# Gated heads of a two-stage transformer: level products on square tiles in column groups, inner levels through a compact table

## The reference

```python
def step(state, inp):
    qc, kc, vc, gc = inp
    bc = jnp.cumsum(gc, axis=2)
    diff = bc[:, :, :, None, :] - bc[:, :, None, :, :]
    decay = jnp.exp(jnp.where(causal, diff, -jnp.inf))
    scores = jnp.einsum('bhtd,bhsd,bhtsd->bhts', qc, kc, decay)
    o = jnp.einsum('bhts,bhsv->bhtv', scores, vc) + jnp.einsum('bhtd,bhdv->bhtv', qc * jnp.exp(bc), state)
    ...
```

## Time and profile before

| | before |
|---|---|
| median of 3 runs | 1345.93 us (1345.53 to 1348.4) |
| the profiled execution: its time | 1350.12 us |
| its span in the trace | 1348.4 us |
| mean granted TensorE clock | 0.95 of full speed |
| TensorE matmul busy | 1187.3 us, 88% |
| VectorE busy | 471.7 us, 35% |
| ScalarE busy | 262.1 us, 19% |
| GpSimd busy | 324.0 us, 24% |

### The profile page before, as it was taken

How to read it: one execution, slowest core, us unless ns; L and a number is a source line. 1 busy time by engine, 2 the same in 40 slices (tenths; PEclk the granted TensorE clock), 3 DMA queues, 4 the chain that set the end, 5 groups by cost and what they waited for, 6 DMA issues and landing times.

```text
span 1348.4 us, 18316 instructions
## 1 busy us (share of the span) xinstructions
PE 1187.3 (88%) x7432; PEld 778.2 (58%) x7438; DVE 471.7 (35%) x1186; ACT 262.1 (19%) x668; POOL 324.0 (24%) x347
## 2 busy tenths in 40 slices
PE   7999999896845666676899999999999999999997
PEld 6874545362512121221476679998458566999843
DVE  3443713110101010110225654444673225444467
ACT  4313431010000000000235532111012322211100
POOL 5000100000000000000102339878001113987800
PEclk9999998997978787887999999999999999999999
DMA  9643377999999999999986036444542057644400
GB/s 349 202 178 125 119 281 275 418 429 425 427 428 427 428 428 429 430 426 422 396 306 214 21 125 219 160 154 157 178 150 78 1 193 244 219 155 159 157 0 31
DMA packets 101357, 335.82 MB, mean 249 GB/s; under 512 B 6728, under 2 KB 58240, under 8 KB 87069
## 3 DMA queue, kind: packets, MB, share of 16 engines
q1 hardware_dynamic: 98662, 326.33, 62.9%
q0 software_dynamic: 2416, 8.30, 1.7%
q10 hardware_dynamic: 199, 0.06, 0.0%
HBM read 333.59 MB, written 2.86 MB: 250 GB/s over the span
## 4 chain that ended last, share of the span: by engine, by line
PE 71%; DMA 18%; DVE 3%; POOL 3%; issue 2%; SPq 1%; ACT 1%; POOLq 0%; DVEq 0%; ACTq 0%
PE bank L1752 18%; PE bank L905 17%; DMA arena<-in_w_expert_up 13%; PE bank L1802 8%; PE bank L1283 5%; DMA wide_rows<-in_w_expert_gate 4%; PE bank L1301 3%; PE bank L1910 2%; PE bank L1171 2%; PE bank L1723 2%; PE bank L1564 2%; PE bank L1537 1%; PE bank L1077 1%; PE bank L1925 1%; DMA ring<-in_w_expert_down 1%
## 5 line engine op out<-in xcount | busy, mean ns | idle before, releaser
L1752 PE MATMUL bank<-R,arena 128*128 128x128 f32 x1056 | 125.1, 275 | 0.0
L1752 PEld LDWEIGHTS bank<-R,arena 128*128 128x128 f32 x1056 | 121.5, 192 | 0.0
L1283 PE MATMUL bank<-ring,arena 128*32 128x512 f32 x512 | 76.0, 684 | 50.7 <-DMA ring<-in_w_expert_up 38.6
L905 PE MATMUL bank<-wide_rows,ring 128*128 128x256 f32 (+1 forms) x512 | 115.5, 384 | 0.0
L2750 DVE TENSOR_TENSOR arena<-arena,bank 64x512 f32<-64x512 f32 x16 | 11.1, 692 | 298.2 <-ACT arena L2166 298.2
L1283 PE MATMUL bank<-wide_rows,arena 128*32 128x512 f32 x128 | 69.5, 695 | 51.6 <-DMA arena<-in_w_expert_up 39.2
L3268 POOL COPY arena<-w_router 128x256 f32<-128x256 f32 x1 | 0.4, 397 | 473.4 <-PE bank L1283 473.4
L905 PEld LDWEIGHTS bank<-wide_rows,ring 128*128 128x128 f32 x512 | 96.1, 190 | 16.0 <-issue 2.1
L1752 PE MATMUL bank<-wide_rows,ring 128*128 128x128 f32 x704 | 91.2, 275 | 1.5 <-ACT wide_rows L2151 1.5
L1752 PEld LDWEIGHTS bank<-wide_rows,ring 128*128 128x128 f32 x704 | 84.7, 192 | 2.5 <-ACT wide_rows L2151 2.5
L1802 PE MATMUL bank<-arena 128*128 128x512 f32 x176 | 81.4, 593 | 0.5 <-DVE arena L3131 0.5
(11 more groups left out here) (410 smaller groups left out, 1973.5 us busy)
## 6 DMA issues: line engine op xcount, KB each, us to landing
ring<-in_w_expert_down SPq DMA_DIRECT2D x29, 2048.0 KB, 16.9
ring<-in_ffn_w_in SPq DMA_DIRECT2D x44, 1024.0 KB, 8.3
ring<-in_w_expert_gate SPq DMA_DIRECT2D x16, 2048.0 KB, 25.2
ring<-in_w_expert_up SPq DMA_DIRECT2D x16, 2048.0 KB, 33.6
arena<-in_w_expert_up SPq DMA_DIRECT2D x14, 2048.0 KB, 32.4
ring<-in_ffn_w_out SPq DMA_DIRECT2D x10, 2048.0 KB, 7.8
ring<-in_w_in SPq DMA_DIRECT2D x7, 2048.0 KB, 16.0
arena<-in_w_expert_gate SPq DMA_DIRECT2D x7, 2048.0 KB, 26.8
```

The costliest lines, as they stand in the source:

```text
L905: last = pe.matmul(dst, lhsT, rhs, start=k == 0, stop=k == len(pairs) - 1)
L1283: last = pe.matmul(bank[e % 2][at:at + SLOTS, :], xg_tile(e % 2, k)[:, SLOTS * r:SLOTS * r + SLOTS], w[r][:, kk, :], start=k == 0, stop=k ...
L1752: last = pe.matmul(up_banks[layer][u % 4][i][:, at * P:(at + 1) * P], weights(k), columns(k), start=k == 0, stop=k == KT // 2 - 1)
```

## The change

Levels 0 and 1 compute only the kept squares. At level 0 each of the 8 tables is one 64x64 matmul; the two chunks go to the two halves of the PSUM partitions (column groups of 64). At level 1 there are 16 matmuls of 32x32 in two of four column groups. From level 2 on, each table is computed as its four 32x32 squares on the diagonal, one for each column group: 32 matmuls of 32x32 a level. All results of a level fit one bank, so a level is one job and not two.

VectorE copies level 0 and 1 straight to `score` (two plain copies each, 64 or 32 rows by 256), and the others with one `copy_predicated` of 128x256 into a compact table `near_score`, through a compact mask. `near_score` lies in the memory of `S0`. After level 7 GpSimd spreads it to its place in `score` (four copies of 32 rows by 256) and signals `mask_ready` 4, for which `hg_outputs` and ScalarE's copy into `S0` now wait. GpSimd also builds the compact mask and clears `near_score` at the start, before `mask_ready` 1.

```diff
@@ plan_jobs
         if what == "level":
-            j.add(f"level{i}", "V", 2)
+            j.add(f"level{i}", "V", 1)
@@ tiles
+        near_mask = take(8 * SLOTS // 4).bitcast(U8).rearrange("p (l t) -> p l t", t=SLOTS)
+        near_score = S0.rearrange("p (c t) -> p c t", t=SLOTS)[:, 0:8, :]
@@ level_products
-                for i in range(2):
-                    b = to_fill(pe, f"level{level}", i)
-                    for c in range(4):
-                        h, tb = (4 * i + c) // 2, c % 2
-                        cut = slice(tb * P, (tb + 1) * P)
-                        if level < 7:
-                            left = right = lev[level % 2][:, h, cut]
-                        else:
-                            left, right = hgk[:, h, META + tb * P:META + (tb + 1) * P], hgq[:, h, cut]
-                        last = pe.matmul(b[:, c * P:(c + 1) * P], left, right, start=True, stop=True)
-                    last.then_inc(job_done, 1)
+                b = to_fill(pe, f"level{level}")
+                factors = lev[level % 2]
+                for h in range(HG_HEADS):
+                    for tb in range(TB):
+                        c = 2 * h + tb
+                        if level == 0:
+                            last = pe.matmul(b[64 * tb:64 * tb + 64, 64 * h:64 * h + 64], factors[:, h, tb * P:tb * P + 64],
+                                             factors[:, h, tb * P + 64:tb * P + P], start=True, stop=True)
+                            continue
+                        for g in range(0, 4, 2 if level == 1 else 1):
+                            at = tb * P + SLOTS * g
+                            left, right = factors[:, h, at:at + SLOTS], factors[:, h, at:at + SLOTS]
+                            if level == 1:
+                                right = factors[:, h, at + SLOTS:at + 2 * SLOTS]
+                            elif level == 7:
+                                left, right = hgk[:, h, META + at:META + at + SLOTS], hgq[:, h, at:at + SLOTS]
+                            last = pe.matmul(b[SLOTS * g:SLOTS * (g + 1), SLOTS * c:SLOTS * (c + 1)], left, right, start=True, stop=True)
+                last.then_inc(job_done, 1)
@@ hg_outputs
                 pe.wait_ge(hg_fac, 10)
+                pe.wait_ge(mask_ready, 4)
@@ ScalarE, other
                 elif what == "s0":
+                    act.wait_ge(mask_ready, 4)
@@ level_scores
-                for i in range(2):
-                    b = filled(dve, f"level{level}", i)
-                    count_emptied(dve.copy_predicated(score[:, 4 * i:4 * i + 4, :],
-                                                      level_mask[:, level:level + 1, :].broadcast_to([P, 4, P]),
-                                                      b[:, :].rearrange("p (a t) -> p a t", t=P)))
+                b = filled(dve, f"level{level}")
+                if level == 0:
+                    for tb in range(TB):
+                        last = dve.tensor_copy(score[0:64, :, :].rearrange("p (h b) t -> p h b t", b=TB)[:, :, tb, 64:P],
+                                               b[64 * tb:64 * tb + 64, 0:T].rearrange("p (h t) -> p h t", t=64))
+                elif level == 1:
+                    for g in (0, 2):
+                        rows = slice(SLOTS * g, SLOTS * (g + 1))
+                        last = dve.tensor_copy(score[rows, :, SLOTS * (g + 1):SLOTS * (g + 2)],
+                                               b[rows, 0:8 * SLOTS].rearrange("p (c t) -> p c t", t=SLOTS))
+                else:
+                    last = dve.copy_predicated(near_score, near_mask[:, level:level + 1, :].broadcast_to([P, 8, SLOTS]),
+                                               b[:, 0:8 * SLOTS].rearrange("p (c t) -> p c t", t=SLOTS))
+                count_emptied(last)
@@ GpSimd, at the start
+            for g in range(4):
+                rows = slice(SLOTS * g, SLOTS * (g + 1))
+                step(pool.tensor_copy(near_mask[rows, :, :], level_mask[rows, :, rows]))
+            step(pool.memset(near_score, 0.0))
             pool.memset(score[:, :, :], 0.0).then_inc(mask_ready, 1)
@@ GpSimd, after the distance DMAs and before gated_squares(0)
+            def near_scores_spread():
+                wait_emptied(pool, "level7")
+                for g in range(4):
+                    rows = slice(SLOTS * g, SLOTS * (g + 1))
+                    last = pool.tensor_copy(score[rows, :, rows], near_score[rows, :, :])
+                    if g < 3:
+                        step(last)
+                last.then_inc(mask_ready, 1)
+                pool.wait_ge(mask_ready, 4)
```

More of the change, by code:

```diff
@@ L2502, in _ @@
                     else:
-                        dve.wait_ge(job_done, jobs.number(f"level{level - 1}", 1) + 1)
+                        dve.wait_ge(job_done, jobs.number(f"level{level - 1}") + 1)
                     level_args(level + 1)
@@ L2516, in _ @@
                              own_head.unsqueeze(2).broadcast_to([P, SB_HEADS, SB_D]), ALU.mult))
-            dve.wait_ge(job_done, jobs.number("level6", 1) + 1)
+            dve.wait_ge(job_done, jobs.number("level6") + 1)
             dve.tensor_copy(lev[0][:, :, :], bcum[:, :, :]).then_inc(hg_arg, 1)
@@ L3242, in gated @@
                 pool.tensor_tensor(rows, rows, hgg[:, tb, :], ALU.mult).then_inc(gated_normed, 1)
+            near_scores_spread()
             gated_squares(0)
```

## The result

The changed kernel takes 1339.85 us (median of 4 runs, 1339.65 to 1341.56), the kernel before beside it 1347.16 us. The ratio is 0.994, 95% interval 0.9923 to 0.9957: by the ratio 8 us faster, by the two medians 7.3. It was measured again on another occasion, with 0.9932 (0.9917 to 0.9948). No change was forecast: 1345.7 us, in a range from 1340.3 to 1351.5. The rival that the array sets the pace had 0.20, with 5.4 us at its first value and 8 us at its outer one.

A forecast was written before the change was run, and what follows sets the result against it. TensorE was taken to bound the stretch; levels 0 and 1 saving 0.99 and 0.86 us, levels 2 to 6 costing 1.60 and level 7 0.01 gave -0.24 us, from 1345.93 to 1345.7, range 1340.3 to 1351.5.

The forecast's parts named there:

- What bounds the stretch: 60 to 100 us: TensorE alone counts; VectorE, ScalarE and GpSimd costed at nothing, VectorE's factors 1.3 us early.
- A shift reaches the end one to one: Time won or lost at 50 to 105 us passes whole through the experts' weight stream, which starts with TensorE.
- (d): Rival: something after 105 us takes up the shift, 1345.9 us; shares the chance of 0.53 with the forecast.
- The change of form: TensorE between full-width projections and narrow levels: 0.11 us going in, 0.20 coming out, 0.31 for each of levels 0 to 6.
- The array's time: TensorE's own time at 15 ns a record: levels 0 and 1 0.48 us each, every other level 0.96.
- The feed: Sequencer to TensorE, levels from 2 on: 34 of 128 instructions lie ready, 94 arrive at 18.5 ns, 1.74 us.
- The arithmetic of the sum: TensorE's levels: level 0 0.99 us less, level 1 0.86 less, levels 2 to 6 1.60 more, level 7 nothing; -0.24.
- (a): Rival, chance 0.20: the array, not the feed, paces the levels; 5.4 us faster, 1340.6, or about 8 at 8 ns.
- (b): Rival, chance 0.20: the levels' instruction feed is slower when it must last, 28 ns each; 5.4 us slower, 1351.3.
- (c): Rival, chance 0.07: thin level matmuls make TensorE's clock fall for 7 us, costing about 3.5 us: 1349.2.

The follow-up runs named there:

- light copies: The kernel before, with VectorE's masked copies of the levels cut to 16 of 128 columns of each table: 1347.07 us, ratio 0.9999.
- fourfold run: The changed kernel with the matmuls of levels 2 to 7 issued four times over, 512 instructions a level: 1377.53 us, ratio 1.0222.
- single burst: The changed kernel with the matmuls of level 4 alone issued four times, one burst of 512 instructions: 1347.95 us, one run.
- Group by group: The changed kernel with the loops of levels 1 to 7 turned, all matmuls of one column group before the next: 1345.96 us, ratio 0.9994.
- three runs with more instructions: The changed kernel with matmuls issued four times (levels 2 to 7), four times (level 4 alone), twice (levels 2 to 7): 1377.53, 1347.95, 1345.7 us.

## Why the prediction was wrong

**What bounds the stretch** was right. TensorE alone counts, VectorE's saving became idle time (light copies: ratio 0.9999), GpSimd's spread and mask were hidden. The slack between VectorE's factors and TensorE stayed at 1.25 us.

**A shift reaches the end one to one**: right, as far as single executions can tell. 37.4 us at `sbvs` became 37.7 by the medians and 35.7 by the spans in the fourfold run; 7.2 became 7.7 in the table above. That also rules out (d).

**The change of form**: right in size. 0.31 us a level were predicted; 0.17 on the way out are in the chain, and 0.69 - 0.57 = 0.12 on the way in.

**The array's time** was a term of the sum that was mis-sized. 15 ns a record was read from records that move 64 columns; with 32 they take 9, and the 8 ns of the earlier trace rows were the nearer row. 64 records take 0.57 us and not 0.96.

**The feed** is the step that failed. It was read at 18.5 ns for each instruction, from 0.6 us between two semaphore waits, and it made a level from 2 on 2.10 us. The level takes 0.69. The reading of the 34 to 36 instructions that lie ready was sound: at the same place of the changed kernel the sequencer passes the same waits 3.1 us into the same job (54.6 after 51.45). But the 95 that did not lie ready were handed over in 0.51 us, 5.3 ns each, and the time between two waits of the sequencer was an upper bound that I used as a value. It could only have been a value if nothing else had held the sequencer between them, and I looked only at the first half's bank, not at the second's. At 5.3 ns the 94 instructions of the sum are 0.5 us and not 1.74, no more than the array takes.

**The arithmetic of the sum** with the measured prices: level 0 with 0.61 + 0.19 against 1.78 is 1.0 us less; level 1 with 0.63 + 0.19 against 1.98 is 1.2 less (it follows the narrow distance job, which the sum had overlooked by taking 1.78); levels 2 to 6 with 0.69 + 0.19 are 0.9 less each, 4.5 in all; level 7 ends 0.55 us after the job ahead of it, against 1.98, and with 0.05 more for that job and 0.24 more for the one behind (1.10 against 0.86) it is 1.1 less; a new wait of 0.22 us at `sbvs` takes some of it back. That is the 7.6 us seen. The wait was not predicted: the old level 7 had covered ScalarE's emptying of `sbv2`, and the text asked who waits for the level, not who was hidden behind it.

**The rivals.** (a) came, at its outer value. (b), that the feed is slower when it has to last, was wrong here but exists: not as a pace, but as a stop of 1.4 to 2.5 us after 256 instructions, and from about twice the instructions of this change on. (c) did not happen in the changed kernel, whose granted clock is 1.00 in every 5 us from 50 to 100; it did in the single burst, after two stops. The range ended at 1340.3 although (a)'s outer value, 8 us faster, had been worked out. With the chance of 0.20 for (a) and a single burst as all evidence against it, that outer value belonged inside.

The Trainium skill's figure of 62 ns of sequencer time for each matmul (TensorE: Matmul & The Clock Gate, section "Wait — 56ns, not 53.3ns?") would make 64 records an estimated 4.0 us; here they take 0.57, so it does not hold for this execution. The page gives it for hardware decoding off, and no run here shows which setting this was. Put into the prediction's own sum it gives some 7 us slower, not the 6 that stand there. The same section gives about 25 ns as the least distance between the starts of two matmuls. Group by group they start 27 ns apart, which 32 columns at two cycles explain by themselves; going round the groups they start 9 ns apart, so that floor doesn't hold across column groups.

## What to carry to other kernels

Before a dense matmul is cut into small ones, count instructions and look at how they follow each other: round the column groups, 64 records of 32x32 took 0.57 us, and in one group after the other 1.7, no better than the full product. The time between two events of a sequencer is an upper bound for its pace, to be believed only when every wait between them is known to have been met. And when a job gets shorter, ask which transfer or copy was hidden behind it.

## What the runs showed of the hardware

In the fourfold run TensorE began 256 LDWEIGHTS and MATMUL instructions at 4.1 ns each; in the changed kernel the sequencer handed them over at 5.3 ns. Instructions came in transfers of 16 KB, 256 at a time; in the single burst one every 3.5 us, and never two within 3.3 us in any of the three runs with more instructions. From a transfer's first packet to the next matmul it took 2.2 to 2.9 us. A stream of more than 256 instructions at full rate stopped TensorE for 1.4 to 2.5 us at a time, also with the DMA engines nearly idle, and for 5.4 us once beside a weight transfer. An estimate from the 3.5 us: 14 ns for each instruction in any stretch that lasts. In the single burst the clock fell to 0.50 of full speed after two such stops, under the projection behind them.
